# Gate rows from a small product and two DMAs instead of four transposes, in a gated DeltaNet and sliding-window layer

## The reference

```
g = -jnp.exp(a_log) * jax.nn.softplus(a + dt_bias)
G = jnp.cumsum(gc, axis=-1)                       # per chunk and head
decay = jnp.exp(jnp.where(causal, G[..., :, None] - G[..., None, :], -jnp.inf))
lower = jnp.where(strict, jnp.einsum('bhnid,bhnjd->bhnij', k_beta, kc) * decay, 0.0)
attn_intra = jnp.einsum('bhnid,bhnjd->bhnij', qc, kc) * decay
k_tail = kc * jnp.exp(G[..., -1:] - G)[..., None]
```

## Time and profile before

| | |
|---|---|
| median of 3 runs | 2134.79 us (2132.6 to 2135.01) |
| profiled execution | 2140.69 us, of which the span is 2138.8 us |
| mean granted clock of TensorE | 0.988 |
| PE busy | 1990.7 us, 93% |
| DVE busy | 1670.1 us, 78% |
| ACT busy | 836.7 us, 39% |
| POOL busy | 527.7 us, 25% |

### The profile page before, as it was taken

The page is one execution under the profiler, slowest core; times in us unless marked ns, Lnnn a source line. Parts: engine busy times, 40 slices in busy tenths (PEclk is TensorE's granted clock), DMA queues, the critical chain, the costliest instruction groups (busy, mean ns, idle before and its releaser), DMA issues.

```text
span 2138.8 us, 60953 instructions
## 1 busy us (share of the span) xinstructions
PE 1990.7 (93%) x25094; PEld 1649.5 (77%) x25094; DVE 1670.1 (78%) x5459; ACT 836.7 (39%) x2616; POOL 527.7 (25%) x811
## 2 busy tenths in 40 slices
PE   0289999999999999999999999999999999999995
PEld 0277888888788888888887888888888888888873
DVE  5987788777778877787887778788777878887773
ACT  0544444343444434343443434444343434433332
POOL 0022222222223222222322222232222223222221
PEclk9999999999999999999999999999999999999996
DMA  7200111110111111001111101111111011111001
GB/s 289 85 9 25 43 43 43 43 34 16 38 43 43 43 43 33 29 26 43 43 43 43 33 24 31 43 43 43 43 33 30 25 43 43 43 43 38 29 13 38
DMA packets 35287, 93.01 MB, mean 43 GB/s; under 512 B 9993, under 2 KB 14402, under 8 KB 33986
## 3 DMA queue, kind: packets, MB, share of 16 engines
q1 hardware_dynamic: 35010, 89.12, 13.0%
HBM read 71.28 MB, written 17.83 MB: 42 GB/s over the span
## 4 chain that ended last, share of the span: by engine, by line
PE 57%; DVE 30%; DMA 5%; ACT 5%; issue 3%; SPq 0%; POOL 0%; POOLq 0%; DVEq 0%; ACTq 0%
PE bank L437 26%; PE bank L624 15%; PE bank L452 8%; DVE qkv L911 7%; DVE base_inv L1003 4%; DVE masks L999 4%; DMA x_in<-near_scratch 3%; DVE qkv L909 2%; DVE w_raw L1283 1%; ACT conv_in L682 1%; PE bank L415 1%; DVE rhs L1140 1%; PE bank L568 1%; DMA near_scratch<-masks 1%; DVE small L950 1%
## 5 line engine op out<-in xcount | busy, mean ns | idle before, releaser
L437 PE MATMUL bank<-xt_half,w_raw 128*128 128x128 f16 x15360 | 934.5, 220 | 54.4 <-DVE w_raw L1283 53.9
L437 PEld LDWEIGHTS bank<-xt_half,w_raw 128*128 128x128 f16 x15360 | 892.5, 99 | 77.4 <-DVE w_raw L1283 54.1
L911 DVE SCALAR_TENSOR_TENSOR qkv<-conv_in,cols,qkv 128x128 f32<-128x128 f32 x1152 | 394.7, 386 | 3.5
L444 PE MATMUL bank<-w_raw,xt_half 128*128 128x264 f16 (+1 forms) x1536 | 269.6, 329 | 0.0
L444 PEld LDWEIGHTS bank<-w_raw,xt_half 128*128 128x128 f16 x1536 | 149.5, 98 | 87.9 <-issue 1.9
L624 PE MATMUL bank<-w_o,inv_t 128*128 128x512 f16 x768 | 172.7, 382 | 2.1 <-DVE inv_t L1216 2.1
L624 PE MATMUL bank<-w_o,out_b_half 128*128 128x512 f16 x768 | 171.0, 379 | 0.0
L691 ACT ACTIVATE tanh_c<-qkv 128x512 f32<-128x512 f32 x96 | 60.5, 630 | 281.5 <-DVE qkv L911 281.5
L624 PEld LDWEIGHTS bank<-w_o,inv_t 128*128 128x128 f16 x768 | 74.2, 98 | 86.7 <-DVE inv_t L1216 2.4
L624 PEld LDWEIGHTS bank<-w_o,out_b_half 128*128 128x128 f16 x768 | 73.9, 98 | 83.0
L999 DVE TENSOR_TENSOR masks<-x_in,base_inv 128x60 f32<-128x60 f32 (+14 forms) x480 | 108.4, 226 | 26.3 <-DMA x_in<-near_scratch 13.2
(11 more groups left out here) (217 smaller groups left out, 3388.5 us busy)
## 6 DMA issues: line engine op xcount, KB each, us to landing
x_in<-in_x_dram SPq DMA_DIRECT2D x32, 512.0 KB, 3.3
x_in<-near_scratch SPq DMA_DIRECT2D x32, 512.0 KB
y_out<-in_x_dram SPq DMA_DIRECT2D x32, 512.0 KB, 3.3
out_dram<-y_out SPq DMA_DIRECT2D x32, 512.0 KB, 7.1
w_raw<-in_w_in_dram SPq DMA_DIRECT2D x8, 1024.0 KB, 12.6
w_o<-in_w_out_dram SPq DMA_DIRECT2D x8, 512.0 KB, 13.1
w_raw<-in_w_in_dram SPq DMA_DIRECT2D x8, 384.0 KB, 11.4
w_raw<-in_w_in_dram SPq DMA_DIRECT2D x8, 256.0 KB, 12.6
```

The lines of the kernel that those rows point to most:

```text
L437: last = mm(dst[:, 128 * b:128 * b + 128], w_half[:, c, ws, col:col + 128], xt_half[:, xs, c, :], start=(c == 0 and ws + xs == 0), stop=(c ...
L444: last = mm(dst[:, 0:n_col], xt_half[:, xs, c, :], w_half[:, c, ws, col:col + n_col], start=(c == 0 and ws + xs == 0), stop=(c == NC - 1 a ...
L911: last = v.scalar_tensor_tensor(dst, conv_in[:, b, i:i + TOK], tap, dst, ALU.mult, ALU.add)
```

## The change

The product with `upper` stays, and gets a second one with exchanged operands: `g_tok` as the weights, `upper` as the moving operand, which gives the cumulated gates as rows, 4 x 128, in bank 2. ACT (not the DVE) copies columns and rows out of the bank, the rows into four partitions of `k_sw`. SP stores the rows to DRAM, waits, and loads them, broadcast to 128 partitions, into `decay`. The DVE then forms the decay's argument in place. The four transposes and the wait for `g_cols_used` go from the PE. The order of the scratch semaphores changes with it; the near-block store and load now count on the same two.

```diff
+        g_row = k_sw[0:4, :, :].rearrange("p h n -> p (h n)")
+        g_row_dram = nc.dram_tensor("g_row_scratch", (4, 128), F32, kind="Internal").ap()
...
@@ sync, step
-                    sp.dma_start(near_dram, m_near.rearrange("p h n -> p (h n)")).then_inc(near_stored, 16)
-                    sp.wait_ge(near_stored, (m + 1) * 16)
+                    sp.dma_start(near_dram, m_near.rearrange("p h n -> p (h n)")).then_inc(scratch_stored, 16)
+                    sp.wait_ge(scratch_stored, (2 * m + 2) * 16)
...
                     sp.dma_start(x_in[:, :], x[0, bass.ds((t + 1) * TOK, TOK), :]).then_inc(x_loaded, 16)
+                if proj:
+                    done(sp, g_row_made, t)
+                    sp.dma_start(g_row_dram, g_row).then_inc(scratch_stored, 16)
+                    sp.wait_ge(scratch_stored, (2 * t + 1) * 16)
+                    done(sp, aw_ready, m)
+                    sp.dma_start(decay[:, :, :].rearrange("p h n -> p (h n)"),
+                                 g_row_dram.rearrange("h n -> (h n)").unsqueeze(0).broadcast_to([128, 512])).then_inc(
+                        scratch_loaded, 16)
@@ tensor, gate_columns and step
-                    mm(bank[2][:, 0:4], upper, g_tok, start=True, stop=True).then_inc(g_col_t, 1)
+                    mm(bank[2][:, 0:4], upper, g_tok, start=True, stop=True)
+                    mm(bank[2][0:4, 128:256], g_tok, upper, start=True, stop=True).then_inc(g_col_t, 1)
...
-                done(pe, g_cols_used, m)
-                for h in range(4):
-                    last = nc.tensor.transpose(heads(2)[:, h, :], g_cols[:, h:h + 1].broadcast_to([128, 128]), ident)
-                last.then_inc(g_row_t, 1)
@@ scalar, step
+                def gate_rows():
+                    done(act, g_col_t, t)
+                    done(act, k_rot_ready, t)
+                    f(g_cols[:, 0:4], bank[2][:, 0:4], ACT.Copy).then_inc(g_cols_used, 1)
+                    f(g_row, bank[2][0:4, 128:256], ACT.Copy).then_inc(g_row_made, 1)
...
                     conv_tanh(t, 1)
+                if proj and mix:
+                    gate_rows()
                 if mix:
                     done(act, out_a_raw, m)
...
                     if not mix:
                         w_out_high(3)
+                        gate_rows()
@@ vector, step
-                    done(dve, g_row_t, m)
-                    v.tensor_copy(g_cols[:, 8:12], heads(2)[:, :, TOK - 1]).then_inc(g_last_ready, 1)
+                    dve.wait_ge(scratch_loaded, (2 * m + 1) * 16)
+                    done(dve, exp_cols_ready, m - 1)
+                    v.tensor_copy(g_cols[:, 8:12], decay[:, :, TOK - 1]).then_inc(g_last_ready, 1)
+                    done(dve, g_cols_used, m)
                     done(dve, g_last_ready, m)
                     v.tensor_tensor(g_cols[:, 4:8], g_cols[:, 8:12], g_cols[:, 0:4], ALU.subtract)
-                    done(dve, aw_ready, m - 1)
                     for h in range(4):
-                        last = v.scalar_tensor_tensor(decay[:, h, :], heads(2)[:, h, :], g_cols[:, h:h + 1], neg,
+                        last = v.scalar_tensor_tensor(decay[:, h, :], decay[:, h, :], g_cols[:, h:h + 1], neg,
                                                       ALU.subtract, ALU.add)
...
-                    done(dve, g_col_t, t)
-                    done(dve, exp_cols_ready, m)
-                    v.tensor_copy(g_cols[:, 0:4], bank[2][:, 0:4]).then_inc(g_cols_used, 1)
                     convolve(t, FILL_Q, range(4), qs_ready if mix else None, m)
```

More of the change, by code:

```diff
@@ L229, in build @@
             sem(n) for n in ("gate_link", "soft_arg_ready", "soft_exp_ready", "g_ready"))
-        g_col_t, g_row_t, g_cols_used, decay_arg_ready, decay_ready, exp_cols_ready = (
-            sem(n) for n in ("g_col_t", "g_row_t", "g_cols_used", "decay_arg_ready", "decay_ready",
+        g_col_t, g_row_made, g_cols_used, decay_arg_ready, decay_ready, exp_cols_ready = (
+            sem(n) for n in ("g_col_t", "g_row_made", "g_cols_used", "decay_arg_ready", "decay_ready",
                              "exp_cols_ready"))
@@ L245, in build @@
         mask_turned, mask_link = sem("mask_turned"), sem("mask_link")
-        near_made, near_stored, block_loaded, base_made, base_set = (
-            sem(n) for n in ("near_made", "near_stored", "block_loaded", "base_made", "base_set"))
+        near_made, scratch_stored, scratch_loaded, base_made, base_set = (
+            sem(n) for n in ("near_made", "scratch_stored", "scratch_loaded", "base_made", "base_set"))
         near_masked, near_ready = (Nth(near_made, 2, i) for i in range(2))
@@ L365, in step @@
                     done(sp, xl_ready, t if proj else m)
-                    sp.dma_start(near_dram, m_near.rearrange("p h n -> p (h n)")).then_inc(near_stored, 16)
-                    sp.wait_ge(near_stored, (m + 1) * 16)
+                    sp.dma_start(near_dram, m_near.rearrange("p h n -> p (h n)")).then_inc(scratch_stored, 16)
+                    sp.wait_ge(scratch_stored, (2 * m + 2) * 16)
                     sp.dma_start(x_in[:, 0:BLOCK * 4 * BLOCK],
                                  near_dram.rearrange("(b j) n -> b (j n)", j=BLOCK).unsqueeze(1).broadcast_to(
-                                     [128 // BLOCK, BLOCK, 4 * BLOCK * BLOCK])).then_inc(block_loaded, 16)
+                                     [128 // BLOCK, BLOCK, 4 * BLOCK * BLOCK])).then_inc(scratch_loaded, 16)
                 if proj:
@@ L992, in linked @@
                     dve.wait_ge(base_made, m * (BASE_LINKS + 2) + count)
-                dve.wait_ge(block_loaded, (m + 1) * 16)
+                dve.wait_ge(scratch_loaded, (2 * m + 2) * 16)
                 done(dve, base_set, m)
```

## The result

The changed kernel takes 2151.53 us (median of 4 runs, 2150.19 to 2155.32), the kernel before 2134.48 us in the same series: a ratio of 1.0081, with a 95% interval of 1.0065 to 1.0097. That is +17 us by the ratio, slower. The profiled execution has a span of 2153.2 us against 2138.8, +14.4 us. Where a difference in us stands beside a ratio it is worked out from the ratio; the difference of the two medians can be up to 3 us off from it.

The account below looks back on a forecast made before the run. The PE was taken as the bound, a second chain 0.16 us behind. Added product +6.8, Gram products -1.8, first tile +2.5, last tile +0.2 us: total +7.7 on 2134.8, 2142.5 us; range 2134.5 to 2152.

Parts of the forecast that it names:

- two holds of POOL: Rival at the decay: DVE slots hold two small POOL instructions per tile; +15.8 us, 2150.6 us; chance 0.25.
- What bounds the kernel: At the Gram products: PE only 0.16 us later than a second chain through ACT, POOL and `finish`.
- The added product: On the PE ahead of `fill(2)`: two f32 passes, 0.22 us a tile on both chains, 6.8 us in all.
- the upper bound: For the added PE product: 0.35 us, a moving pass plus an uncovered load of L509's size, twice.
- The alternative given beside it: For the added PE product: new load nearly free, next fill's load hidden; 0.17 us, sum 1.5 us smaller.
- The hold of POOL: At the decay: DVE instructions with two SBUF inputs make POOL wait until they end; one hold, +0.17 us, taken.
- all 0.07 earlier: On the second chain: without the DVE copy L1223, decay slots and POOL instructions all come 0.07 us earlier.
- no hold: Rival at the decay: POOL is never held, needing a 0.2 us shift; +2.4 us, 2137.2 us; chance 0.20.
- the phase of 0.32 us: At the decay: first DVE slot at 2013.97, first small POOL instruction at 14.29, held to 14.46.
- the one-hold case: Main case at the decay: one POOL hold per tile, Gram products 0.06 us earlier; total +7.7 us; chance 0.42.
- ACT and the DMAs in full tiles: Gate copies on ACT, some 0.35 us, and SP's store and load, 1.4 and 2.5 us, cost nothing in full tiles.
- The first tile: At the first decay: the gate rows' load is not hidden; +2.5 us, bounds 1.3 and 6.8 us.

Follow-up runs that it names:

- e2_no_turns: The kernel before without the four gate transposes from the second tile on, the DVE reading a spread PSUM column instead; 2135.63 us, ratio 0.9992.
- e8_full_weights: The kernel before plus one unread product with 128 weight and 128 moving columns behind the column product; 2147.69 us, ratio 1.0051.
- e6_rows_first_tile: The changed kernel with the two gate copies on ACT ahead of the last half of the output weights, first step only; 2149.75 us, ratio 1.0057.
- e9: The changed kernel with m mod 8 small DVE reductions ahead of the four decay instructions, shifting them against POOL; 2153.82 us in one run.
- e10: The kernel before, whose decay reads PSUM, with m mod 8 small DVE reductions ahead of its four decay instructions; 2136.64 us in one run.
- e1: The kernel before plus the unread product with four weight and 128 moving columns behind the column product, transposes kept; 2149.88 us, ratio 1.0059.
- e7: The kernel before with the column product (128 weight, four moving columns) made twice, the second result unread; 2142.75 us, ratio 1.0034.
- v1_combined: The changed kernel with the two small products behind the transposes of x and the gate copies behind Q's convolution-input copy on ACT; 2135.88 us, ratio 1.0002.
- c1_after: The changed kernel, unaltered, measured again on another occasion against the kernel before; 2149.81 us, ratio 1.0067.
- e3: The changed kernel with the row product's weights 64 columns wide (60 of them zeros) in place of four; 2154.5 us, ratio 1.0087.
- e4: The changed kernel with its two small products exchanged, the row product first and then the column product; 2153.72 us, ratio 1.0076.
- e5: The changed kernel with m mod 4 tiny DVE memsets between the subtraction and the four decay instructions; 2152.41 us, ratio 1.0077.

## Why the prediction was right and wrong

The forecast said slower, by 7.7 us; it is slower, by 14 to 17 us. The time lies within the range, but close to its upper end, and that by luck: the range was drawn for two holds of POOL, and there is none. With the terms as the profiles show them the sum is about 8.6 us (2.0 + 6.4 + 0.2 in the table above); the rest was in no term.

**What bounds the kernel: right.** Two chains 0.16 us apart. `e2_no_turns` is the direct test: 0.435 us of PE work removed, 0.11 us gained. The start of L462 0.06 us behind the end of L1247 is there, too. One term was not priced: Gram products that start after a stop take 0.04 us longer (2.05 against 2.00 us).

**The added product: the term that was mis-sized most.** 0.22 us a tile was taken, with 0.35 as the upper bound; it is 0.38, so 31 x 0.16 = 5.0 us too little. The step took the moving width as the whole price, from rows in which all weights are 128 wide. The two full passes cost 0.30 us at this place (`e8_full_weights`) and the narrow weights 0.08 more, since no load is pulled ahead at the two borders. The upper bound had that idea (an uncovered load, twice) but hung it on the 0.145 us of L509, in which the loads do overlap. The alternative given beside it, 0.17 us with a narrow load that is nearly free and the fill's load hidden (the Trainium skill, "TensorE: Matmul & The Clock Gate", LDWEIGHTS), points the wrong way here as a price for the exchange: the load is short, 0.09 us for two, but it lies open, and so does the next one.

**The hold of POOL: the mechanism was right, its place wrong.** The forecast took one hold of 0.17 us a tile and named unchanged lengths of 0.19, 0.19 and 0.56 us as what would refute it; the lengths are unchanged, so by its own test it is wrong in this step. The scans show that the hold exists, and that it is there with the SBUF operand and not with the PSUM one. The step that failed is "all 0.07 earlier": the decay did not keep its place against POOL. L1062 comes 0.27 us behind L1059, where before the subtraction came 0.20 us behind the copy; so the first slot lies 0.25 us ahead of POOL and not 0.32, and each of the three POOL instructions, 0.27 us apart, starts within about 0.02 us of a border between slots 0.26 us apart. It is the case called "no hold", for which the prediction itself asked for a shift of 0.2 us; 0.07 did it. What the phase of 0.32 us would have cost was not run. Whether the added wait or the SBUF source of L1059 makes these 0.07 us was not tried. Without the hold the Gram products come 0.22 us earlier against the transposes of x (11.19 against 11.41 us), 0.01 from the 0.23 of that case; less the 0.04 of the restart that is 30 x -0.18 = -5.4 us in place of -1.8.

**The two errors cancel in part.** +5.0 and -3.6 us: the regular tiles, 11.8 - 5.4 = 6.4 us, look much like the 5.0 us of the forecast, with both terms wrong. That is luck: by the sum alone the one-hold case would seem confirmed; the lengths of three POOL instructions refute it.

**ACT and the DMAs in full tiles: right.** ACT's next copy (L834) starts 1.37 us behind L645, exactly as L819 did behind L638 before, so the gate copies end within a wait that was there already. The store lands in 1.18 us, the load is waited for in the first tile alone.

**The first tile: right in cause.** +2.5 us forecast, +2.0 and +2.3 in the two profiles; these hold one added product, 0.38 us, which the sum counts apart, so 1.6 to 2.0 are left. The DVE starts 150.43 - 148.56 = 1.9 us later, and takes the wait of 2.55 us for the load, which needs 3.2 us and not 2.5 after its issue at 147.25. `e6_rows_first_tile` takes 1.3 to 1.7 us of it back.

**What was not in the sum at all.** The tiles that are longer than the period. The time beyond the period in one profile of each run, but for `e9` and `e10`, in which the period itself changes from tile to tile:

| kernel | beyond the period, us | waits for the block load |
|---|---|---|
| before | 10.2 | 9 |
| `e1` / `e7` / `e8` / `e2` | 8.5 / 4.3 / 5.2 / 4.5 | 7 / 6 / 6 / 8 |
| `v1_combined` | 4.9 | 6 |
| after / `c1_after` | 14.1 / 9.1 | 11 / 9 |
| `e3` / `e4` / `e5` / `e6` | 14.4 / 12.1 / 13.4 / 9.7 | 12 / 11 / 10 / 10 |

The medians of the runs say the same: by their ratios `e1`, `e7` and `e8` come out within 2 us of 30 times their change of the period, the kernels of the last two rows 4 to 9 us above period and first tile together. So some 5 to 8 us of the +14 to +17 are neither in the period nor in the first tile. The table alone doesn't show them, as `c1_after` has less than the kernel before. But the execution profiled before took 2140.69 us, 6.2 above its median. If what an execution takes above its median lies in these tiles, the median execution has about 4 us beyond the period before and about 10 after (14.1 - 3.8 and 9.1 + 0.5); that is an estimate.

What makes such tiles long can be read: the near blocks' store, 1.45 us from its issue to that of the block load, takes 1.6 to 3.7 us in 4 to 8 tiles of each kernel. In the first profile of the changed kernel these tiles hold 12.8 of the 14.1 us, in the kernel before 9.8 of 10.2. One of them, first the issues on SP's queue, then the DMA queue that is named "instruction" (packets, MB, share of 16 engines), from 532.4 to 536 us and over the whole span:

```profile
532.45 0.32 SPq L368 DMA_DIRECT2D near_scratch<-masks  x1
535.92 0.61 SPq L370 DMA_DIRECT2D x_in<-near_scratch  x1
...
q8 instruction: 1, 0.02, 2.2%
...
q8 instruction: 197, 3.23, 0.6%
```

One transfer of that queue, 16 KB, lies in this store's time: it starts 1.09 us behind the store's issue and ends at +2.38, and the block load is issued 1.1 us after that. It is so in all 14 traces. In 89 tiles of 448 the block load is issued more than 1.6 us behind the store; each of the 89 has such a transfer, which starts between 0.7 us before and 1.64 us behind the store's issue, and the block load follows 0.98 to 1.22 us behind its end. Of the stores that have one starting between 0.4 us before and 1.05 us behind their issue, 59 in all, none is fast. So a store is late when a transfer of q8, by its name the program's own code, falls beside it. No run moved the one against the other, so this rests on the timing alone.

Why more of the stores are hit in these kernels stays open. It isn't the two new DMAs as such, since `v1_combined` has them; it isn't the wait at L462, since `e2_no_turns` has it; nor the period of 62.00 us, since `e7_column_twice` has it. What is left is where in time the stores fall against the transfers of code, and no run varied that alone.

The last piece is +0.7 to +2.0 us behind the last K's transposes. 0.4 us of it is that the Gram products start 4.86 us behind these instead of 4.44: without the transposes of the gates K's start earlier, and `finish` still bounds the Gram products there. The rest goes with stretches at the lower clock level, which fall on other instructions (the 16 passes of the Gram products take 3.09 us in the last tile before, 3.54 and 2.48 in the two profiles after, against 2.00 in a full tile); they were not studied.

## What to carry to other kernels

Price an added matmul by the distance between its neighbours, not by its own passes: here a product with fewer weight columns than the stream around it left two loads open that otherwise run ahead, in whichever order the two products stood. Where two chains lie within a few tenths of a microsecond, work that stands ahead of the point where they part costs in full, and work on one of them alone is nearly free up to the gap: with the same two products behind that point and the copies moved the loss is gone, 6 of the 14 us by the period. And where a hold depends on which instruction starts first, work out the phase of each instruction after every edit, the short waits included; 0.07 us moved all three instructions to the borders of slots here.

## What the runs showed of the hardware that was not expected

- **Narrow weights among full ones.** Added price of one f32 product of two passes, from the start of the `mt` product to the fill, against 0.58 us: 128 weight columns and 4 moving +0.22 us; 128 and 128 +0.30; 4 and 128 +0.38; 64 and 128 +0.44; 4 and 128 between full products on both sides, the column product last, +0.51. With 128 columns the next load starts 0.11 us ahead of its matmul, with 4 or 64 at the same time as it.
- **The hold of POOL.** It ends with the DVE's slot of 0.26 us, after which the small POOL instruction needs its last 0.13 us: 0.04 to 0.19 us in five of eight phases (`e9_phases_wide`), none in three; none at eight phases with a PSUM input (`e10_phases_before`).
- **Stores of 32 KB and transfers of code.** A slow store (3.3 to 3.5 us to the next issue) comes at 532.45 and 908.04 us in the first profile of the changed kernel and at 532.47 and 907.14 in the second; the slow ones of one profile lie mostly 5 or 6 tiles apart, some in neighbouring tiles. The transfers of the instruction queue q8, 16 KB each, recur too: in the first profile of the changed kernel 184 lie between 211 and 2060 us, about 6.1 a tile, so they shift against the tile. In each of the 89 slow stores of all traces one of them is under way or starts before the store is through, and the next issue comes 0.98 to 1.22 us behind its end.
